# Seven RMS norms: the sum of squares in one product with ones, the inverse root by logarithm and exponential in the next phase

## The reference

```
def rmsnorm(x, g):
    y = xf * lax.rsqrt(jnp.mean(xf * xf, axis=-1, keepdims=True) + EPS) * g
```

## Time and profile before

| | |
|---|---|
| runs of the kernel before | 3314.62, 3317.59, 3318.62 us |
| span of the profiled execution | 3315.3 us |
| PE busy | 3209.5 us, 97% |
| DVE busy | 1924.1 us, 58% |
| ACT busy | 1440.5 us, 43% |
| mean granted clock of PE | 0.987 |

### The profile page before, as it was taken

The page is one execution under the profiler, slowest core; times in us unless marked ns, Lnnn a source line. Parts: engine busy times, 40 slices in busy tenths (PEclk is TensorE's granted clock), DMA queues, the critical chain, the costliest instruction groups (busy, mean ns, idle before and its releaser), DMA issues. The chain is left out here.

```text
span 3315.3 us, 51847 instructions
## 1 busy us (share of the span) xinstructions
PE 3209.5 (97%) x20772; PEld 2547.2 (77%) x20772; DVE 1924.1 (58%) x3355; ACT 1440.5 (43%) x2349; POOL 56.8 (2%) x44
## 2 busy tenths in 40 slices
PE   8999999999999999999999999999999999899998
PEld 6777788788877777788888888767678788566786
DVE  6544745677557447446775373268756652478555
ACT  6423523444246225334443243455643443656632
POOL 0010000000000210000000000000000000000000
PEclk9999999999999999999999999999999999999999
DMA  4324332333333224432333253223153442132342
GB/s 164 90 79 145 140 115 77 108 96 98 111 128 92 79 60 164 163 99 89 95 99 111 70 185 113 86 77 86 38 191 116 133 149 102 63 97 59 142 145 70
DMA packets 107694, 358.37 MB, mean 108 GB/s; under 512 B 12681, under 2 KB 13065, under 8 KB 104785
## 3 DMA queue, kind: packets, MB, share of 16 engines
q1 hardware_dynamic: 107472, 355.33, 33.5%
HBM read 310.57 MB, written 38.81 MB: 105 GB/s over the span
## 5 line engine op out<-in xcount | busy, mean ns | idle before, releaser
L224 PE MATMUL banks<-h_high,weights_high 128*128 128x512 f32 x2448 | 980.9, 401 | 16.9 <-DVE weights_low L245 11.7
L225 PE MATMUL banks<-h_low,weights_high 128*128 128x512 f32 x2448 | 956.9, 391 | 0.0
L226 PE MATMUL banks<-h_high,weights_low 128*128 128x512 f32 x2448 | 956.9, 391 | 0.0
L224 PEld LDWEIGHTS banks<-h_high,weights_high 128*128 128x128 f32 x2448 | 461.1, 188 | 125.7 <-DVE weights_low L245 13.4
L226 PEld LDWEIGHTS banks<-h_high,weights_low 128*128 128x128 f32 x2448 | 460.9, 188 | 98.0
L225 PEld LDWEIGHTS banks<-h_low,weights_high 128*128 128x128 f32 x2448 | 461.6, 189 | 93.0 <-issue 3.3
L1854 DVE TENSOR_TENSOR weights_low<-ring,weights_high 128x1024 fp32r<-128x1024 f32 (+2 forms) x124 | 164.6, 1328 | 292.1 <-ACT weights_high L1800 292.0
L1800 ACT CAST weights_high<-ring 128x1024 fp32r<-128x1024 f32 (+2 forms) x124 | 140.6, 1134 | 437.2 <-PE banks L226 437.0
L217 DVE TENSOR_TENSOR weights_low<-ring,weights_high 128x1024 fp32r<-128x1024 f32 x131 | 161.9, 1236 | 277.9 <-ACT weights_high L212 276.5
L212 ACT CAST weights_high<-ring 128x1024 fp32r<-128x1024 f32 x131 | 137.2, 1048 | 378.7 <-PE banks L226 373.6
L1998 ACT CAST weights_high<-ring 128x1024 fp32r<-128x1024 f32 (+1 forms) x116 | 132.5, 1142 | 322.6 <-PE banks L226 322.6
(11 more groups left out here) (473 smaller groups left out, 4902.0 us busy)
## 6 DMA issues: line engine op xcount, KB each, us to landing
ring<-in_in SPq DMA_DIRECT2D x136, 512.0 KB, 4.2
ring<-in_up SPq DMA_DIRECT2D x88, 512.0 KB, 3.6
ring<-in_gates SPq DMA_DIRECT2D x72, 512.0 KB, 4.2
x<-in_gates SPq DMA_DIRECT2D x56, 512.0 KB, 4.2
ring<-in_down SPq DMA_DIRECT2D x32, 704.0 KB, 4.1
ring<-in_out SPq DMA_DIRECT2D x32, 512.0 KB, 3.6
ring<-in_branch SPq DMA_DIRECT2D x16, 768.0 KB, 4.3
stored<-g_spill SPq DMA_DIRECT2D x16, 768.0 KB, 4.5
```

Of the source, the lines that this page charges most:

```text
L224: pe.matmul(bank, core.wh[:, half, w], high, start=start, stop=False)
L225: pe.matmul(bank, core.wh[:, half, w], low, start=False, stop=False)
L226: return pe.matmul(bank, core.wl[:, half, w], high, start=False, stop=stop)
```

## The change

The sum over channels is one product: ones (128x128) as the stationary side, the total of all eight squares (128x512) as the moving one. It leaves each token's sum on all 128 partitions, so nothing is spread. DVE adds the last square too. After the barrier ACT makes the inverse root on 128x512 elements as exp(-0.5 ln(mean + eps)), in the place in which it copied. The dummy root becomes a load of the table set that holds both functions. `sum_channels` now stands behind the last block of the ahead product. Between the stacks both means come out of the phase as they are, and the next phase makes both roots, with two more operations on DVE.

```diff
 def sum_channels(pe, sems, core):
-    pe.wait_ge(sems["summed"], KD - 2)
-    pe.wait_ge(sems["squared"], KD)
-    for c in range(NCH):
-        t = slice(c * CH, (c + 1) * CH)
-        for n in (2, (KD - 1) % 2):
-            mm = pe.matmul(core.banks[7][:, c:c + 1], core.squares[:, n, t], core.ones[:, 0:1], start=(n == 2), stop=(n != 2))
-    mm.then_inc(sems["sum_steps"], 1)
+    pe.wait_ge(sems["summed"], KD - 1)
+    pe.matmul(core.banks[7][:, :], core.ones[:, :], core.squares[:, 2, :], start=True, stop=True)
...
 def take_root(act, sems, core):
-    act.wait_ge(sems["sum_steps"], 1)
-    act.activation(core.by_token[:, 0:NCH], core.banks[7][:, 0:NCH], ACT.Sqrt, bias=core.eps[:, 0:1], scale=1.0 / D)\
-        .then_inc(sems["rooted"], 1)
...
+    act.activation(core.root[:, :], core.banks[7][:, :], ACT.Ln, bias=core.eps[:, 0:1], scale=1.0 / D).then_inc(sems["root_logged"], 1)
+    act.wait_ge(sems["root_logged"], 1)
+    act.activation(core.root[:, :], core.root[:, :], ACT.Exp, scale=-0.5).then_inc(sems["root_ready"], 1)
...
+def take_both_means(act, sems, core, last):
+
+    act.activation(last, core.banks[7][:, :], ACT.Ln, bias=core.eps[:, 0:1], scale=1.0 / D).then_inc(sems["root_logged"], 1)
+    act.wait_ge(sems["root_logged"], 1)
+    act.activation(core.root[:, :], last, ACT.Exp, scale=-1.0).then_inc(sems["last_inverted"], 1)
...
+    dve.tensor_tensor(core.banks[6][:, :], core.banks[6][:, :], core.root[:, :], ALU.mult).then_inc(sems["second_scaled"], 1)
...
+    act.activation(core.root[:, :], core.banks[6][:, :], ACT.Ln, bias=core.eps[:, 0:1], scale=1.0 / D).then_inc(sems["root_logged"], 1)
...
+    dve.tensor_tensor(core.root[:, :], core.root[:, :], last, ALU.add).then_inc(sems["logs_joined"], 1)
...
+    act.wait_ge(sems["logs_joined"], 1)
+    act.activation(core.root[:, :], core.root[:, :], ACT.Exp, scale=-0.5).then_inc(sems["root_ready"], 1)
+    act.activation(last, last, ACT.Exp, scale=-0.5).then_inc(sems["last_ready"], 1)
...
         if k == 3:
-            act.wait_ge(sems["spread"], 1)
-            act.copy(core.root[:, :], core.banks[7][:, :]).then_inc(sems["root_ready"], 1)
+            if last is None:
+                take_root(act, sems, core)
+            else:
+                take_both_means(act, sems, core, last)
+        if k == 6 and last is not None:
+            log_second_mean(act, sems, core)
+    if last is not None:
+        take_both_roots(act, sems, core, last)
     if not first:
         act.wait_ge(sems[LANDED[1]], 16)
         high_part(act, sems, core, (1, KD * P), 1)
...
             if ahead is not None:
                 pe.wait_ge(sems["x_added"], KD - 1)
-                ahead_products(pe, sems, core, ahead, count + KD, 0, KD - 1)
+                ahead_products(pe, sems, core, ahead, count + KD, 0, KD)
             sum_channels(pe, sems, core)
-            if ahead is not None:
-                ahead_products(pe, sems, core, ahead, count + KD, KD - 1, KD)
...
-                    warm_root(act, core)
+                    act.preload_act_table_set(LOG_AND_EXP)
...
-            invert_root(dve, sems, core)
+            sum_tile(dve, sems, core, KD - 1)
```

More of the change, by code:

```diff
@@ L424, in opening_round, with opening_split @@
         high_part(act, sems, core, (1, KD * P), 1)
-def opening_split(dve, sems, core, gain, high, low, first=0):
+def opening_split(dve, sems, core, gain, high, low, first=0, last=None):
     if first:
@@ L438, in opening_split @@
             other_low(dve, sems, core, slot(core, first, KD * P), first)
+        if k == 5 and last is not None:
+            scale_second_mean(dve, sems, core)
+    if last is not None:
+        join_logs(dve, sems, core, last)
     if not first:
```

117 lines of the change are left out of this document (38 added, 79 removed).

## The result

The changed kernel is slower by a little: a median of 3321.77 us over 12 runs (3315.40 to 3325.12) against 3318.19 (3311.93 to 3320.87) for the kernel before in the same comparison, a ratio of 1.0016 (95% interval 1.0008 to 1.0023). Two later comparisons of the same two kernels gave 1.0015 (1.0006 to 1.0024) and 1.0027 (1.0017 to 1.0038). A ratio is not the quotient of the two medians and differs from it by up to 0.0008 (here the quotient is 1.0011). The profiled execution took 3322.04 us.

The account below looks back on a forecast made before the run. PE, 97% busy, was taken to bound the kernel, with ACT feeding DVE bounding the openings. Seam terms summed to -2.1 us, a span of 3313.2; the median lies 2.3 above, so 3315.5, range 3311.5 to 3319.5 (8 in 10).

Parts of the forecast that it names:

- The sum side: Norm sums at seven seams: eight products become one, a gain of 0.95 us at ahead seams, 1.2 to 3.4 at others.
- the dear end of its bounds: Between the stacks, PE's last product was to end between 1903.1 and 1905.0 us; the later end.
- The root side: Five openings, not between the stacks: logarithm and exponential replace a copy, 0.8 us more on ACT in the bounding chain.
- Hidden openings: Rival: PE at low clock hides the added 0.8 us at four of five seams; -4 to -6.6 us, chance 0.13.
- The opening between the stacks: Second tile 4.5 us later against a barrier 3.4 earlier: net +1.1 us, with PE idle about 3 us.
- The clock at more seams: Rival: longer PE idling lowers the clock at six more seams, 1.7 us each, +8 in all, 3325.7; chance 0.06.
- The added loads: A table load of 1.28 us before `project2`'s root in both second layers, covered by ACT's idle time, counted as nothing.
- the change doesn't do what it says: Rival: the loaded table set not in force at the first logarithm, adding 7 x 2 loads of 1.28 us, +18.
- The sum: Step adding the net terms of all seams: -2.1 us against the profiled span, giving 3313.2 us.
- something unseen on the faster side: Whole kernel: a gain beyond -6.6 us, together with something the prediction didn't see; chance 0.07.

Follow-up runs that it names:

- one_op_root: Changed kernel with one ACT operation writing ones instead of logarithm and exponential, in five openings and at the end, not between the stacks: 3316.11 us, ratio 1.0001.
- fill_gap: Changed kernel with three dead 128x512 products in PE's wait for the second weight tile between the stacks: 3320.57 us, ratio 1.0011 to the kernel before.
- cast_first: Changed kernel with the second weight tile's high and low part between the stacks put ahead of the two exponentials and sum of logarithms: 3320.34 us, ratio 1.0007.
- again: Changed kernel with no edit, measured and profiled a second time: 3321.97 us, ratio 1.0015 to the kernel before.
- again2: Changed kernel with no edit, in a later comparison: 3326.55 us, ratio 1.0027 to the kernel before.
- before_again: Kernel before, unchanged, profiled once more in one run: second rwkv phase 288.47 us; no total time is given.
- refill3: Changed kernel with PE's instruction count restored up to the second rwkv phase by dead products, none at the start of branch phases: 3318.75 us, ratio 1.0001.

## Why the prediction was wrong

It said 3315.5 us, 2.1 under the kernel before, and most likely within 0.2% of it, in a range of 3311.5 to 3319.5; the kernel took 3321.8, 0.16% slower. That is inside the 0.2%, but 2.3 us above the range and to the other side: the interval 1.0008 to 1.0023 leaves out 1, and the forecast was 0.9994.

- *The sum side* held. The start is 1.0 to 1.7 us shorter over the executions in the table, with the product at 2.04 us; the first merge is 1.03 shorter where no low clock fell into it (0.95 forecast), and 0.08 and 0.25 where 3.4 us did; the product behind a dense block takes 1.02. Between the stacks PE's last product ended 4.1 us behind ACT's last square, the dear end of its bounds, so ACT opened 2.7 earlier against that square (7.39 before, 4.70 now), not 3.4.
- *The root side* held: the second tile's low part ends 0.74 to 0.76 us later behind the opening in all five (8.73, 9.21, 8.73, 9.20 and 9.21 before), 0.8 forecast, and `one_op_root` took 0.66 or 0.67 of it away. Hidden openings, the rival that would have made it faster, did not come.
- *The opening between the stacks* held to 0.1 us (13.66 against 13.8, PE idle 3.00 against "about 3"). The term was mis-sized by the clock: I priced a wait of PE at its length, and it cost 2.8 us more, by which `fill_gap` shortened the phase. That the phase behind was 3.3 us shorter (78.73 to 75.40, with 3.4 us of low clock instead of 13.7) made the net of the seam, 661.9 to 663.5 us over the three phases in the table around it (means of two and three executions), 1.6 against the forecast 1.1. That the net came out near the forecast is luck: two clock terms that it didn't have nearly cancelled. They are not one cost handed on, for `fill_gap` took away the first and kept the second, although `cast_first` lost both. Why that phase had less low clock I don't know.
- *The clock at more seams* did not come at the size that this rival needed: the low stretches behind the start sum to 82.5, 92.7 and 72.3 us in the profiled executions of after, `again` and `again2`, and to 87.6 and 84.6 in those of before and `before_again`. Single seams did change: the clock fell in the first feed-forward opening of after (597.9 us) and `again2` and not in before. Nor did such a stretch cost what I put down, 1.7 us for 3.4: in the first merge it cost 0.8 to 1.0. The Trainium skill ("TensorE: Matmul & The Clock Gate", "What's actually happening") has the clock follow how busy the engine has been; the seam between the stacks agrees, with 0.50 behind the wait and 1.00 where `fill_gap` filled it.
- *The added loads* are hidden. The one in project2 stands ahead of its root, and ACT is idle behind it (timeline of ACT, after):

```profile
1978.08 1.28 ACT L2704 ACT_TABLE_LOAD   x1
1979.37 0.69 ACT L2704 ACTIVATE root<-banks,eps 128x512 f32<-128x512 f32 x1
...
1981.96 1.05 ACT L213 CAST weights_high<-ring 128x1024 fp32r<-128x1024 f32 x1 [1.90 <-PE banks L227]
```

The Trainium skill ("ScalarE: Activation LUTs", "What ACT_TABLE_LOAD costs") adds a drain of about 1.38 us to the load's 1.28. The load's 1.28 agrees; the drain doesn't show here, as the activation starts 0.01 behind the load's end, and the load 0.02 behind the copy ahead of it. After has 71 loads where before has 69, the two of these rows and no other, so none stands in the openings, and the rival that the change doesn't do what it says fell.

- *The step that failed is "The sum".* It adds up seven seams and takes every stretch between them as unchanged. The removed instructions were priced by their duration alone, and one effect of removing them has no duration at its place: from about 150 to 267 us behind the last of them, PE runs out of instructions. The second rwkv phase is 5.8 us longer (mean of three, 294.3, against 288.5), of which the opening explains the 0.7 that is left in `refill3` (289.24). The remaining 5.1 is most of the 6.3 by which the prediction missed; in the measured time it is some 4 us by the estimate at one clock. With the number of instructions restored (`refill3`, 1.0001, 0.9992 to 1.0010) the forecast's 0.9994 lies inside the interval. I had left 0.07 for something unseen on the faster side, and almost nothing on the slower one.

What stays open: what makes a packet late, and why the same place costs nothing in one execution and 0.4 to 1.0 us in another; why the named waits sum to 1.0 to 1.6 us less than the phase lies over `refill3`'s; why 124 dead instructions in the kernel before brought back only 2.8 us; and part of the runs' scatter, which goes with the clock (runs of the kernel before have mean clocks from 0.985 to 0.990, and the lower the longer). The mean of the clocks is 0.9877 over 103 runs of the kernel before and 0.9864 to 0.9870 in the three sets of the changed one. At 2.2 us for 0.001 that is an estimated 1.5 to 2.9 us of the measured difference, and whether the change lowers the clock or chance did is not shown.

## What to carry to other kernels

When PE is near 100% busy, read its waits for "issue" in the stretches of the smallest products before and after any edit: taking out instructions anywhere ahead can lengthen such a stretch by several us, in a phase that the edit doesn't touch. Count PE's instructions up to each such wait: if the counts differ by multiples of 256, as here, the waits stand at the ends of packets, and as many dead instructions as were taken out, put where PE waits anyway, show whether that is the cause. Price a new wait of PE at its length plus what the clock takes behind it. And compare phase by phase between barriers, not by the total: gains and losses of 1 to 7 us in single phases made up a difference of 4.

## What the hardware showed that I had not expected

- Stretches with products of 64x64 can outrun PE's supply of instructions: waits of 0.3 to 2.2 us each, within a phase at whole multiples of 256 instructions from each other (16348, 18140, 18907, 20699, 21211, to within one), each ending 2.2 to 2.6 us after a 16 KB packet of q8 began, and gone or moved when some 130 instructions are added far ahead.
- A semaphore increment on PE is not free: 132 took 19.9 us, 0.15 each. One-column matrix instructions took 0.20 each in an opening (22 in 4.46 us), and 0.115 each behind dense products (16 in 1.84).
- A 3.00 us wait in an opening was followed by 6.8 us at a granted clock of 0.50, and filling the same wait with dense dead products kept it at 1.00.
